# A mixture of experts on gathered blocks of 128 token slots, in order of count, with results scattered to DRAM rows

## The reference, cut to what matters

```python
g_top, g_idx = lax.top_k(group_prob, 1)
e_top, e_idx = lax.top_k(exp_prob, TOP_K)            # TOP_K = 2 of 4 in the group
comb = one_hot(g_idx) * (g_top * within)             # 256 tokens x 16 experts, 2 of 16 not zero
for gi in range(N_GROUPS_2):
    hg = jnp.einsum('td,edf->tef', xf, w_gate[gi])   # 1024 -> 512
    hu = jnp.einsum('td,edf->tef', xf, w_up[gi])
    act = jax.nn.silu(hg) * hu * comb[:, gi, :, None]
    out = out + jnp.einsum('tef,efd->td', act, w_down[gi])   # 512 -> 1024
```

## Time and profile before

| what | before |
|---|---|
| median of three runs | 2129.5 us (2129.39 to 2129.65) |
| the profiled execution, its time | 2127.98 us |
| its span in the profile | 2126.2 us |
| part before the first matmul of an expert | 1554.7 us |
| experts, to the last matmul | 562.8 us |
| tail | 8.7 us |
| TensorE busy, share of the span | 98% |

### The profile page before, as it was taken

How to read it: one execution, slowest core, us unless ns; L and a number is a source line. 1 busy time by engine, 2 the same in 40 slices (tenths; PEclk the granted TensorE clock), 3 DMA queues, 4 the chain that set the end, 5 groups by cost and what they waited for, 6 DMA issues and landing times.

```text
span 2126.2 us, 33308 instructions
## 1 busy us (share of the span) xinstructions
PE 2076.1 (98%) x13696; PEld 1894.4 (89%) x13696; DVE 1228.9 (58%) x1238; ACT 913.8 (43%) x920; POOL 49.5 (2%) x58
## 2 busy tenths in 40 slices
PE   8999999999999999999999998999989999999998
PEld 8998989999999888888899988888879999999997
DVE  5666665665544666635556667655665555555555
ACT  4434344344343545534443355344543443333343
POOL 1000000000000000011000010310000000000000
PEclk9999999999999999999999999999999999999999
DMA  7776456774555455556377743423525555555552
GB/s 230 251 248 211 141 176 199 250 250 152 179 185 189 141 196 181 176 93 106 104 228 242 241 141 121 159 89 111 177 96 194 184 191 178 180 191 181 181 191 82
DMA packets 268800, 372.96 MB, mean 175 GB/s; under 512 B 11800, under 2 KB 212878, under 8 KB 268704
## 3 DMA queue, kind: packets, MB, share of 16 engines
q1 hardware_dynamic: 265920, 363.04, 52.0%
q0 software_dynamic: 2800, 8.79, 2.9%
HBM read 370.66 MB, written 1.12 MB: 175 GB/s over the span
## 4 chain that ended last, share of the span: by engine, by line
PE 90%; DVE 5%; ACT 3%; issue 1%; DMA 1%; SPq 0%; ACTq 0%; DVEq 0%; POOLq 0%
PE ps L325 27%; PE ps L327 27%; PE ps L326 27%; PE ps L949 2%; DVE lo L308 1%; PE ps L971 1%; ACT hi L302 1%; PE ps L959 1%; ACT w L390 1%; PE ps L1409 1%; PE ps L1397 1%; PE ps L920 0%; PE ps L1407 0%; PE ps L691 0%; PE ps L409 0%
## 5 line engine op out<-in xcount | busy, mean ns | idle before, releaser
L308 DVE TENSOR_TENSOR lo<-raw,hi 128x2048 fp32r<-128x2048 f32 x320 | 732.3, 2293 | 570.7 <-ACT hi L302 570.6
L302 ACT ACTIVATE hi<-raw 128x2048 fp32r<-128x2048 f32 x320 | 611.1, 1914 | 611.2 <-PE ps L327 608.2
L325 PE MATMUL ps<-xT_hi,hi 128*128 128x256 f32 x2752 | 783.7, 285 | 12.9 <-DVE lo L308 7.7
L326 PE MATMUL ps<-xT_lo,hi 128*128 128x256 f32 x2752 | 781.7, 284 | 0.0
L327 PE MATMUL ps<-xT_hi,lo 128*128 128x256 f32 x2752 | 781.4, 284 | 0.0
L325 PEld LDWEIGHTS ps<-xT_hi,hi 128*128 128x128 f32 x2752 | 531.0, 193 | 18.0 <-DVE lo L308 8.1
L326 PEld LDWEIGHTS ps<-xT_lo,hi 128*128 128x128 f32 x2752 | 531.2, 193 | 3.3 <-issue 0.2
L327 PEld LDWEIGHTS ps<-xT_hi,lo 128*128 128x128 f32 x2752 | 531.1, 193 | 0.0
L325 PE MATMUL ps<-hi,xT_hi 128*128 128x512 f32 x544 | 216.4, 398 | 7.2 <-ACT gr L1567 2.6
L327 PE MATMUL ps<-hi,xT_lo 128*128 128x512 f32 x544 | 212.1, 390 | 0.0
L326 PE MATMUL ps<-lo,xT_hi 128*128 128x512 f32 x544 | 211.9, 390 | 0.0
(11 more groups left out here) (357 smaller groups left out, 1701.9 us busy)
## 6 DMA issues: line engine op xcount, KB each, us to landing
raw<-in_ffn_w_in SPq DMA_DIRECT2D x176, 512.0 KB, 4.7
raw<-in_ffn_w_out SPq DMA_DIRECT2D x88, 512.0 KB, 4.2
raw<-in_attn_w_qkv SPq DMA_DIRECT2D x72, 512.0 KB, 4.7
raw<-in_w_in SPq DMA_DIRECT2D x64, 512.0 KB, 4.5
raw<-in_w_gate SPq DMA_DIRECT2D x64, 512.0 KB, 3.6
raw<-in_w_up SPq DMA_DIRECT2D x64, 512.0 KB, 4.5
raw<-in_w_down SPq DMA_DIRECT2D x64, 512.0 KB, 3.9
modraw<-in_mod_w SPq DMA_DIRECT2D x48, 512.0 KB, 6.4
```

The costliest lines, as they stand in the source:

```text
L302: nc.scalar.activation(hi[u % SPLIT][:, :], raw[u % RAW][:, :], ACT.Copy).then_inc(S("hi_ready"), 1)
L308: nc.vector.tensor_tensor(lo[u % SPLIT][:, :], raw[u % RAW][:, :], hi[u % SPLIT][:, :].bitcast(F32), ALU.subtract).then_inc(S("lo_ready"), 1)
L325: nc.tensor.matmul(dst, w_hi, x_hi, start=start, stop=False, skip_group_check=True)
L326: nc.tensor.matmul(dst, w_hi, x_lo, start=False, stop=False, skip_group_check=True)
```

## The change

The program to the end of the mixer stays as it was, but for three things: the buffers `raw` and `h` stand at the top of SBUF, TensorE's start of the layer behind the first feed-forward part also waits for `rows_zeroed`, and POOL writes zeros to 512 DRAM rows `expert_rows` (four DMAs of 512 KB, issued behind its first ones).

The experts are new code without a loop. A **step** n handles one expert: position 0 is expert 0, with all 256 tokens (2 blocks); positions 1 to 15 are the others in order of their token counts (`order`, found on the chip; SP reads the expert's number from SBUF with `value_load` before its loads). Positions 1, 6 and 11 (`DOUBLE`) get the three largest experts with two blocks of 128 slots, the others one block: 20 blocks of 128 in all, where there were 16 x 2. For each block now the tokens are held (128x128) and the weights move, 512 columns at a time: 48 matmuls for gate and up, 24 for down. POOL writes 0/1 matrices `pick` (L2144), and TensorE gathers the tokens of two blocks (a batch) with them: eight `fill`s of four matmuls of 256 columns, each copied out of PSUM by ScalarE (even ones, to `xg_hi`) or VectorE (odd ones, to `xg_lo`) in `gathered`. The fills of a batch stand in the units of the steps before it (`FILLED_IN`), from batch 2 on all in one bank, 7. The hidden values are turned by four transposes (`turn`), split again (`inner_hi`, `inner_lo`), and the result of a block is copied (`y_copy`) and written to `expert_rows` at row numbers in `dest` by an indexed DMA of POOL (`bounds_check`: slots without a token write nothing). Each token has two rows there. At the end SP reads the rows back, VectorE adds them, and expert 0 and the last one come through PSUM.

```diff
-        raw = [sb(f"raw{i}", [P, UNIT]) for i in range(RAW)]
...
+        raw = [sb(f"raw{i}", [P, UNIT]) for i in range(RAW)]
...
+        DOUBLE = {1: 0, 6: 1, 11: 2}
...
+        SINGLES = [n for n in range(1, N_POS) if n not in DOUBLE]
+        RANK = {n: DOUBLE[n] if n in DOUBLE else len(DOUBLE) + SINGLES.index(n) for n in range(1, N_POS)}
...
+        for _n in range(N_POS):
+            BLOCKS[_n] = (N_BLOCKS, N_BLOCKS + 1) if _n == 0 or _n in DOUBLE else (N_BLOCKS,)
+            N_BLOCKS += len(BLOCKS[_n])
+        _u = U0["moe"]
+        for _n in range(N_POS):
+            GUU[_n] = _u
+            _u += 4
+            if _n >= 2:
+                DNU[_n - 1] = (_u, _u + 1)
+                _u += 2
+        LAST = N_POS - 1
+        DNU[LAST], DNU[0] = (_u + 1, _u + 2), (_u, _u + 3)
...
+        BATCH_OF = {n: (BLOCKS[n][0] - 2) // 2 for n in range(1, N_POS)}
+        FILLED_IN = {}
+        for _n in range(1, N_POS):
+            _m = BATCH_OF[_n] + 1
+            if _m < N_BATCH:
+                for _i in range(4):
+                    _u = GUU[_n] + _i
+                    if _n == 1:
+                        FILLED_IN[_u] = [(_m, _f) for _f in range(3 * _i, min(3 * _i + 3, 8))]
+                    elif len(BLOCKS[_n]) == 2:
+                        FILLED_IN[_u] = [(_m, 2 * _i), (_m, 2 * _i + 1)]
+                    else:
+                        FILLED_IN[_u] = [(_m, 4 * (BLOCKS[_n][0] % 2) + _i)]
...
+            for n in range(1, N_POS):
+                b, w = BLOCKS[n][0] - 2, P * len(BLOCKS[n])
+                for t in range(TT):
+                    place = slot_of[:, t, RANK[n]:RANK[n] + 1]
+                    nc.gpsimd.tensor_scalar(pick[:, t, b * P:b * P + w], slot_no[:, 0:w], place, None, ALU.is_equal).then_inc(S("picked"), 1)
...
+            for i, b in enumerate(Y_ORDER):
+                pool.wait_ge(S("y_copied"), 2 * (i + 1))
+                pool.indirect_dma_start(moe_rows.ap(), bass.IndirectOffsetOnAxis(dest[:, b - 2:b - 1], 0), ysb[i % 2][:, :],
+                                        None, bounds_check=2 * T - 1, oob_is_err=False).then_inc(S(f"y_stored{i % 2}"), 16)
...
+            for n in range(N_POS):
+                if n == 1:
+                    sp.wait_ge(S("order_ready"), AT["order_ready"] + 1)
+                if n:
+                    expert[n] = sp.value_load(order[0:1, RANK[n]:RANK[n] + 1], min_val=1, max_val=EXPERTS - 1)
+                for i in range(4):
+                    load_in(n, i)
+                if n >= 2:
...
+            for i in range(2):
+                sp.wait_ge(S(f"y_stored{i}"), 16 * len(Y_ORDER[i::2]))
+            for c in range(2):
+                for t in range(TT):
+                    r = (c * TT + t) * P
+                    sp.dma_start(y_back[:, t, c, :], moe_rows.ap()[r:r + P, :]).then_inc(S(f"y_loaded{t}"), 16)
...
+            def y_copy(b):
+                i = Y_ORDER.index(b)
+                if b in ODD:
+                    act.wait_ge(S("y_odd"), ODD.index(b) + 1)
+                else:
+                    wait_used(act, DNU[[n for n in BLOCKS if b in BLOCKS[n]][0]][1])
+                if i >= 2:
+                    act.wait_ge(S(f"y_stored{i % 2}"), 16 * (i // 2))
+                for c in range(2):
+                    nc.scalar.activation(ysb[i % 2][:, c * 512:c * 512 + 512], ps[:, y_bank(b) + c, :], ACT.Copy).then_inc(S("y_copied"), 1)
...
+            for n in range(1, N_POS):
+                for i in range(4):
+                    u = GUU[n] + i
+                    if n == 1 and i < 2:
+                        continue
+                    for m, f in FILLED_IN.get(u - 3, ()):
+                        gathered(m, f)
+                    if n == 2 and i == 2:
+                        silu(1)
+                    if n >= 3:
+                        if i == 0:
+                            silu(n - 1)
+                        if i == 2 and n >= 3 and n - 2 in DOUBLE:
+                            y_copy(BLOCKS[n - 2][1])
+                        if i == 3:
+                            if n - 2 >= 1:
+                                y_copy(BLOCKS[n - 2][0])
+                            if n - 1 >= 2:
+                                inner_hi(BLOCKS[n - 1][0])
...
+            def gathered(m, f):
+                if f % 2:
+                    dve.wait_ge(S("fill_lo_mm"), fill_no(m, f))
+                    nc.vector.tensor_copy(xg_lo(m)[:, f - 1:f + 1, :].rearrange("p k s -> p (k s)"), ps[:, fill_bank(m, f), :]).then_inc(S("fill_lo"), 1)
...
+            def fill(m, f):
+                if f == 0:
+                    pe.wait_ge(S("picked"), 2 * max(n for n in BATCH_OF if BATCH_OF[n] == m))
+                if m == 1:
+                    pe.wait_ge(S("fill_lo" if f % 2 else "fill_hi"), 4 + f // 2)
+                elif m:
+                    i = 8 * m + f
+                    pe.wait_ge(S("fill_hi"), (i + 1) // 2)
+                    pe.wait_ge(S("fill_lo"), i // 2)
+                elif f >= 4:
+                    pe.wait_ge(S("fill_lo" if f % 2 else "fill_hi"), f // 2 - 1)
+                k0, src = f - f % 2, xtok_lo if f % 2 else xtok_hi
+                for k in range(2):
+                    for t in range(TT):
+                        last = nc.tensor.matmul(ps[:, fill_bank(m, f), k * T:k * T + T], src[:, t, (k0 + k) * P:(k0 + k) * P + P],
+                                                pick[:, t, m * T:m * T + T], start=k == 0 and t == 0, stop=t == TT - 1,
+                                                skip_group_check=True)
+                last.then_inc(S("fill_lo_mm" if f % 2 else "fill_hi_mm"), 1)
...
+            def gate_up_unit(n, i):
+                u = GUU[n] + i
+                pe_wait_unit(pe, u)
+                w_hi, w_lo = (x[u % SPLIT][:, :].rearrange("p (k g f) -> p k g f", k=2, g=2) for x in (hi, lo))
+                if n == 0:
+                    x_hi, x_lo = xT_hi, xT_lo
+                else:
+                    m = BATCH_OF[n]
+                    x_hi, x_lo = xg_hi(m), xg_lo(m)
+                    if i == 0:
+                        pe.wait_ge(S("fill_hi"), 4 * m + 4)
+                        pe.wait_ge(S("fill_lo"), 4 * m + 4)
+                fills = list(FILLED_IN.get(u, ()))
+                order = [(b, k) for b in BLOCKS[n] for k in range(2)] if i == 3 else [(b, k) for k in range(2) for b in BLOCKS[n]]
+                for j, (b, k) in enumerate(order):
+                    if i == k == 0:
+                        if b >= 2:
+                            pe.wait_ge(S("e_prod"), b - 1)
+                        if b - 2 in ODD:
+                            wait_y_copied(pe, b - 2)
+                    ss, kk = slice((b % 2) * P, (b % 2) * P + P), 2 * i + k
+                    for g in range(2):
+                        last = product(ps[:, gu_bank(b) + g, :], x_hi[:, kk, ss], x_lo[:, kk, ss], w_hi[:, k, g, :], w_lo[:, k, g, :],
+                                       kk == 0, kk == KT - 1)
+                    if fills and (n == 1 or j in (0, 2)):
+                        fill(*fills.pop(0))
+                last.then_inc(S("pair_used"), 1)
...
+            def down_unit(n, i):
+                u = DNU[n][i]
+                pe_wait_unit(pe, u)
+                w_hi, w_lo = (x[u % SPLIT][:, :].rearrange("p (k n) -> p k n", k=2) for x in (hi, lo))
+                blocks = sorted(BLOCKS[n], reverse=True)
+                if i == 0:
+                    pe.wait_ge(S("e_lo"), BLOCKS[n][-1] + 1)
+                    if n >= 2:
+                        wait_y_copied(pe, BLOCKS[n - 1][0])
+                for b, k in [(b, k) for b in blocks for k in range(2)] if i else [(b, k) for k in range(2) for b in blocks]:
+                    f, o_hi, o_lo = 2 * i + k, inner(e_hi, hid0_hi, b), inner(e_lo, hid0_lo, b)
+                    for c in range(2):
+                        cs_ = slice(c * 512, c * 512 + 512)
+                        last = product(ps[:, y_bank(b) + c, :], o_hi[:, f, :], o_lo[:, f, :], w_hi[:, k, cs_], w_lo[:, k, cs_], f == 0, f == 3)
+                    if f == 3 and b in ODD:
+                        last.then_inc(S("y_odd"), 1)
+                last.then_inc(S("pair_used"), 1)
...
+            gate_up_unit(0, 0)
...
+            for n in range(2, N_POS):
+                for i in range(4):
+                    gate_up_unit(n, i)
+                    if n == 2 and i < 2:
+                        turn(2 + i)
+                    if n > 2 and n - 1 in DOUBLE and i == 0:
+                        turn(BLOCKS[n - 1][1])
+                    if n == LAST - 1 and i == 1:
+                        last_turn()
+                down_unit(n - 1, 0)
+                down_unit(n - 1, 1)
+                turn(BLOCKS[n][0])
+            pe.wait_ge(S("back_ready"), AT["back_ready"] + 1)
+            first_down_unit(0)
+            down_unit(LAST, 0)
+            down_unit(LAST, 1)
```

555 lines of the change are left out of this document (418 added, 137 removed).

## The result

The changed kernel takes 1994.0 us (median of three executions; 1993.0 to 1997.7), against 2129.6: a ratio of 0.9369, 95% interval 0.9352 to 0.9386, 134 us less. The forecast was 1979.3 in 1955 to 2012, so the time lies in the range, but outside the 1968 to 1990 that had half of the chances. The profiled execution took 1993.04 with a span of 1991.2; the forecast's sum gave a span of 1976, so it was 15 us short.

A forecast was written before the change was run, and what follows sets the result against it. TensorE's matmul columns were taken as the bound. Experts start at 1554.7; opening and steps reach 1940.5; from gate and up's end at 1934.5, 41.5 more give a 1976 span, and 1.8 plus 1.5 make 1979.3 us, range 1955 to 2012.

The forecast's parts named there:

- the ring: Weight buffers' circle of load, round and split; forecast to be last only in steps 14 and 15, 9.0 us a round.
- The opening: From the experts' start at 1554.7 to step 1's first gate-up matmul at 1587.8, with about 6 us of waits.
- Step 1: Step of position 1: wide matmuls, 8 fills, 8 transposes, 36 tiny matmuls and 2 us for the clock, 31.2 us.
- E: Rival: TensorE needs more than 0.2267 us for 512 columns with operands turned about; given nothing apart.
- One-block steps: Seven steps (3, 4, 5, 8, 9, 10, 13): 20.3 us each, including a 1.45 us wait for a fill copy.
- Steps 14 and 15: Last two steps, without fills: the ring is last, 18.0 us each; 18.8 by the skill page's bandwidth.
- The end: From the last expert's gate and up (1934.5) through indexed write, read-back and six VectorE passes to the span's end: 41.5 us.
- Costed at nothing: Zeros, places of `raw` and `h`, `value_load` from step 2 on, and the results' DMA work: no time added.
- A: Rival: the ring bounds all one-block steps, +32 us, 2011, half of it likelier, 1995; chance 0.25.
- B: Rival: no waits of fills, 18.8 us a one-block step, and the read-back hidden: 1955; chance 0.10.
- C: Rival: POOL's picks end at 1602 if splits shut it out, 1621 at twice the price; 0.12 with similar opening delays.
- D: Rival: indexed result writes hold everything if one exceeds 30 us, slower than before; chance of slower or unchanged 0.03.

The follow-up runs named there:

- e10: Changed kernel with ScalarE's silu for step 1's first block waiting only for that block's own last matmul, not the whole unit: ratio 0.9346 to the kernel before.
- e9: Changed kernel with most single edits together (copy order, small steps early, short matmuls spread, first product early, two end passes), ranks left in place: ratio 0.9282 to before.
- e1: Changed kernel with VectorE copying the second fill ahead of the fourth unit's split in one-block steps: ratio 0.9336 to the kernel before.
- e3: Changed kernel with about half of the weight loads left out from step 2 on: ratio 0.9336 to the kernel before.
- e7: Changed kernel with sixteen routed blocks in place of eighteen, only position 1 having two: ratio 0.9222 to the kernel before.
- e11: Changed kernel with both e1's earlier fill copy and e3's halved weight loads: ratio 0.9294 to the kernel before.
- e2: Changed kernel with the first block's hidden values made before the fourth unit's other work on ScalarE and VectorE: ratio 0.9369 to the kernel before.
- e6: e4 plus rank matmuls behind position 0's first unit, and step 1's first unit rounded and split ahead of the token copies: ratio 0.9354 to the kernel before.
- e4: Changed kernel with VectorE's 14 small steps on weights and destinations moved ahead of its wait for the rank matmuls: ratio 0.9360 to the kernel before.
- e5: Changed kernel with the router's 48 short matmuls and step 1's 36 tiny ones spread between wide ones: ratio 0.9349 to the kernel before.
- e8: Changed kernel with two VectorE passes in place of six on the rows read back at the end: ratio 0.9368 to the kernel before.

## Why the prediction was nearly right, step by step

The mechanism was right: TensorE bounds the experts, a fill waits for one copy, the ring takes the last two steps, VectorE's passes on rows read back set the end. The sizes of several terms were not. The 15 us are these (steps are counted here as in the forecast, to the end of a turn, so step 2 is 0.5 longer than in the table above):

| term | forecast | measured | off by |
|---|---|---|---|
| first matmul of step 1 | 1587.8 | 1593.35 | +5.6 |
| step 1 | 31.2 | 36.8 | +5.6 |
| step 2 | 26.8 | 26.9 | +0.1 |
| one-block steps 3, 4, 5, 8, 9, 13 | 20.3 | 20.0 to 20.6 | -0.2 |
| step 10 | 20.3 | 21.8 | +1.5 |
| steps 6, 11 | 31.6 | 31.6, 32.1 | +0.5 |
| steps 7, 12 | 26.7 | 27.1, 27.4 | +1.1 |
| steps 14, 15 | 18.0 | 18.9, 19.7 | +2.6 |
| end, from 6.0 ahead of the last turn's end | 41.5 | 39.9 | -1.6 |

*The opening* failed at its first sentence, "Experts start at 1554.7". The router's product is turned about as well: 48 matmuls of 20 columns in 5.6 us where 24 of 256 took 3.8 (1550.88 to 1554.71), so the first wide one stands at 1557.44. That is 1.8 us. Another 0.9 is the part ahead, which began the router at 1551.84 and not 1550.88; in other executions it was 1549.93 to 1552.33, on both sides of the changed kernel's, so this part varies by more than the 0.9 and a small cost of the zeros can't be told from it. 1.5 went to the clock in the first two units (12.4 for 10.9), and about 1.4 to the 14 small steps, 4.2 us in place of 2.8. `order` came 3.6 us behind the ranks where 3.2 were assumed, and the register read as assumed: `order` at 1573.4, SP's first load 1574.5.

*Step 1* had three terms wrong. The 36 tiny matmuls took 4.07 and not 2.5 (the bound of 4.3 was the better value). The clock cost about 2.2 us behind the stop (the first six wide matmuls took 2.7 us, not 1.4) and 1.7 behind the tiny ones, where I had 2 for both. And a wait was missing: step 2's first matmul waits 1.56 for step 1's product, since no down unit lies between them (e10). The rest of the sum was nearly right: e9's step 1, with the clock at 1.00 and a wait of only 0.2, took 31.8, where the sum without its 2 for the clock and with 4.1 for the tiny ones gives 30.8. Most of that 1.0 is the spacing of the wide matmuls (E below).

*One-block steps* were right within 0.3, and so was the place of the wait (e1, e3); it is 1.0 where the ring is ahead and 1.2 to 1.4 where it is not quite.

*Steps 14 and 15* are bound by the ring as said (e3), but two rounds of it take 19.3 and not 18.0. The mis-sized term is the 4.5 for a unit's transfer: from its first issue to the landing of its second load a unit took 4.8 to 7.1 us there, 5.3 in the median of eleven. The loads did not keep up:

```profile
1918.12:1936.97 18.85, 17.84 (x79) 13.93 (x78) 14.42 (x8) 12.12 (x11) 1.42 (x1) 1.00 0.91 314
1936.97:1956.70 19.73, 18.19 (x78) 13.56 (x76) 15.02 (x9) 14.21 (x11) 1.42 (x1) 1.00 0.92 333
```

314 and 333 GB/s over 19 us, where I had reasoned from 416 in one. The Trainium skill, DMA: Bandwidth & Descriptors, section Bandwidth, has about 358 GB/s for a core, from which the prediction gave 18.8 for each of these steps. The trace agrees with the page better than with my choice; that it is this limit and not the ring's own round trip, no run here tells apart.

*The end* is off by only 1.6 because errors cancel. The chain of the changed kernel has the last indexed write, and the read-back of the first tile:

```profile
1962.33 3.02 DMA expert_rows<-ysb,dest
...
1966.21 6.29 DMA y_back<-expert_rows
```

ScalarE had copied the last result 10.3 us from the starting point, as forecast. The write was taken from the earlier trace rows at 6.5. The sixteen before it did take 6.3 in the median, but this last one, issued at 1962.33, 0.3 us ahead of the landing of the last weights, took 3.0. So the read-back began 3.2 earlier than forecast; its first tile took 7.1 and not 6.5 (no run shows the 380 GB/s of that term), the six passes the 7.5 of the forecast, and the rest 11.1 and not 10.2.

*Costed at nothing*: the zeros and the places of `raw` and `h` cost nothing that the trace shows (1519.79 and 1520.68 us of TensorE ahead of the experts).

*The rivals.* A: its halved price, 1995, is the measured time, but by luck. The ring does not bound the seven steps (e3), and of the 15 us missing only some 4 are the ring's (steps 10, 14 and 15); most of the others are in the opening and step 1. In all 8.2 us of the experts are the ring's (e3), and it takes a part of whatever is gained (e1, e7). B: its 18.8 is what e1 and e11 gave once the copy was moved. C: POOL was done at 1604.2, 13 us ahead of need, and near the 1602 that the rival had for passes shut out by VectorE's splits. That is what happened. The 5.9 ns an element (32 passes in 28.6 us) are not a price of the comparison: a pass of 128x128 took 0.59 us and one of 128x256 0.92, but the three that met splits took 2.95, 5.0 and 2.6, some 8 us more in all (row of the passes with their least, median and greatest ns; the 5.0 began at 1584.89):

```profile
L2144 POOL TENSOR_SCALAR pick<-slot_no,by_rank x30: 591/597/5039, 1575.5 to 1602.4; 128x128 fp32r<-128x128 f32 x24, 128x256 fp32r<-128x256 f32 x6
...
1584.73 4.49 DVE L339 TENSOR_TENSOR lo<-raw,hi 128x2048 fp32r<-128x2048 f32 x2
```

D: no write held TensorE up; the last one stands in the chain of the end, as forecast. E: nearly nothing, but not quite. Wide matmuls of the down units were 0.227 us apart, as the earlier trace rows says, those of gate and up 0.227 to 0.231 with the tokens in `xT` and 0.232 to 0.235 with them in `xg` (steps 6 and 11; medians). That is the 0.5 us between these two steps, and some 0.7 in step 1. Why the tiles differ, no run tells.

## What to carry to other kernels

When a product's operands are turned about, look for its small uses too: a helper that becomes better for 512 columns makes 48 short matmuls of 24 longer ones elsewhere, and in or behind a dense row of short ones the clock fell here although TensorE was busy. Put such matmuls between wide ones. A wait of 2 to 3 us can cost more than itself in the same way: where the clock fell behind one, some 1.7 us went as well (e7). When a wait is traced to an operation that stands too far behind in an engine's queue, check the queues of both engines that feed it (e2), and never put a wait on a transfer ahead of work that is ready (e6, e9). An idle stretch that one edit fills can be closed by another (e4 and e5, in e9). Where two engines' limits lie within 5% of one another, the gain of an edit is what the second leaves of it: measure each alone and both together (e1, e3, e11).

## What was not expected of the hardware

The clock fell to 0.50 (1.2 GHz) in or behind 48 matmuls of 20 columns and behind 36 of 4 columns, with TensorE busy in every microsecond from 1552 to 1564 and from 1617 to 1627, and stayed at 1.00 in e5 with the same matmuls spread. In e8 it fell 2 us into the first row already. TensorE had waited 2.05 us some 5 us ahead of the router; it had in the kernel before too, whose router has 24 matmuls of 256 columns and kept 1.00. So the short matmuls are needed for the fall, and whether that wait helps it is open. How long the clock stayed low differed between executions of one code (3.2 us of time). Behind single waits it fell in some executions (2.1 to 3.1 us, in e2, e5, e6, e7 and e10) and not in others (2.8 us, step 10 of the changed kernel).

VectorE and POOL slowed one another. POOL's comparisons stood still for the length of VectorE's splits (2.0 us more beside one split of 2.29, 4.1 beside two in 4.49), while the splits took what they take anywhere. VectorE's small steps were slower while POOL compared: 14 of them took 4.16 us at 1580.5 beside POOL, and 3.05 in e9 ahead of POOL's first pass, with every other one or so at twice its time. The Trainium skill, SBUF — State Buffer, section SBUF: two separate sides, has VectorE and POOL take one shared port pair in turn, for whole instructions, when VectorE reads two operands from SBUF and POOL reads SBUF too, or when VectorE works in a mode that uses two ports. The trace agrees for the splits, which have two operands in SBUF and held POOL up for 8 us in all; that the same rule slows the small steps, no run shows.
